# Weighting expert rows before an accumulating scatter, with a reordered router and double-buffered exponentials

## What is computed

```python
# differential attention: 4 heads, two 64-wide score maps each, 1024 keys
w = softmax(q1 @ k1.T * scale) - lam * softmax(q2 @ k2.T * scale)
o = rms_norm(w @ v, g_sub) * (1 - lam_init)
...
h = h + concat([oa, ob]) @ w_out
# mixture of experts: 32 experts in 4 groups, the best 2 of the best group for each token
a = rms_norm(h, g_ffn)
weights, experts = route(a @ w_rg, a @ w_re)          # [1024, 2]
y_e = (silu(a_e @ w1[e]) * (a_e @ w3[e])) @ w2[e]     # w1, w3: 1024x512, w2: 512x1024
h = h + sum over the two slots of weights * y_e
h = h + rms_norm(p @ w_ple, g_ple) * sigmoid(rms_norm(h, g_plg) @ w_plg)
# then two hybrid layers (retention and stick-breaking attention) and a last norm
```

## Time and profile before

| | us |
|---|---|
| median of 3 runs | 3491.62 (3491.36 to 3495.02) |
| profiled execution, its own time | 3490.98 |
| its span in the trace | 3489.2 |
| TensorE busy | 2927.1 (84%) |
| VectorE busy | 1540.2 (44%) |
| ScalarE busy | 1222.0 (35%) |
| GpSimd busy | 298.2 (9%) |

### The profile page before, as it was taken

One profiled execution on the slowest core, in us unless ns is written; L12 is line 12 of the kernel. 1 busy time (PEld: TensorE's weight loads), 2 busy tenths in 40 slices (PEclk: granted clock), 3 DMA queues, 4 the chain that ended last, 5 costly groups with the idle time before them and its releaser, 6 DMA issues. The chain is left out here.

```text
span 3489.2 us, 61320 instructions
## 1 busy us (share of the span) xinstructions
PE 2927.1 (84%) x22494; PEld 2278.4 (65%) x22494; DVE 1540.2 (44%) x2880; ACT 1222.0 (35%) x2193; POOL 298.2 (9%) x489
## 2 busy tenths in 40 slices
PE   7997875886966999999477999868877999868876
PEld 6785654665854888888365888754466888754455
DVE  3852666777222221222344421168844421058853
ACT  4332544666031110101243222258832222148841
POOL 0001641000002111111100000000000000000000
PEclk9998997898967999999788999979998999979988
DMA  5114543211346999999755222341044221160034
GB/s 181 66 72 162 136 129 105 63 35 65 99 147 225 386 394 393 392 394 395 249 189 175 94 96 72 121 141 34 10 157 160 103 99 72 66 205 19 25 121 163
DMA packets 246492, 541.80 MB, mean 155 GB/s; under 512 B 29904, under 2 KB 112656, under 8 KB 221680
## 3 DMA queue, kind: packets, MB, share of 16 engines
q1 hardware_dynamic: 216832, 460.21, 37.1%
q0 software_dynamic: 28544, 79.99, 6.9%
q10 hardware_dynamic: 1008, 0.20, 0.0%
HBM read 433.46 MB, written 107.79 MB: 155 GB/s over the span
## 5 line engine op out<-in xcount | busy, mean ns | idle before, releaser
L509 PE MATMUL ps<-in_wh,in_xh 128*128 (+1 forms) x1024 | 401.0, 392 | 0.0
L511 PE MATMUL ps<-in_wh,in_xl 128*128 (+1 forms) x1024 | 399.5, 390 | 0.0
L510 PE MATMUL ps<-in_wl,in_xh 128*128 (+1 forms) x1024 | 399.4, 390 | 0.0
L509 PEld LDWEIGHTS ps<-in_wh,in_xh 128*128 128x128 f32 x1024 | 193.1, 189 | 40.0
L510 PEld LDWEIGHTS ps<-in_wl,in_xh 128*128 128x128 f32 x1024 | 193.0, 188 | 39.8
L511 PEld LDWEIGHTS ps<-in_wh,in_xl 128*128 128x128 f32 x1024 | 192.8, 188 | 40.1
L1061 DVE TENSOR_TENSOR ex_hid<-ps,ex_act 32x128 f32<-32x128 f32 x96 | 28.2, 294 | 325.4 <-PE ps L1108 324.5
L509 PE MATMUL ps<-mix_in_wh,mix_in_xh 128*128 (+1 forms) x384 | 152.1, 396 | 9.0 <-DVE mix_in_out L426 5.4
L510 PE MATMUL ps<-mix_in_wl,mix_in_xh 128*128 (+1 forms) x384 | 149.9, 390 | 0.0
L511 PE MATMUL ps<-mix_in_wh,mix_in_xl 128*128 (+1 forms) x384 | 149.8, 390 | 0.0
L275 ACT COPY in_out<-ps 128x512 f32<-128x512 f32 x64 | 37.5, 587 | 249.0 <-PE ps L511 249.0
(11 more groups left out here) (408 smaller groups left out, 7318.9 us busy)
## 6 DMA issues: line engine op xcount, KB each, us to landing
ex_w_w1a<-in_w_dram SPq DMA_DIRECT2D x32, 1024.0 KB
ex_w_w1b<-in_w_dram SPq DMA_DIRECT2D x32, 1024.0 KB
ex_w_w3a<-in_w_dram SPq DMA_DIRECT2D x32, 1024.0 KB
ex_w_w3b<-in_w_dram SPq DMA_DIRECT2D x32, 1024.0 KB
ex_w_w2a<-in_w_dram SPq DMA_DIRECT2D x32, 1024.0 KB
ex_w_w2b<-in_w_dram SPq DMA_DIRECT2D x32, 1024.0 KB, 14.3
proj<-in_out SPq DMA_DIRECT2D x128, 256.0 KB, 2.0
da_w_ada<-in_w_ada_dram SPq DMA_DIRECT2D x32, 768.0 KB, 4.3
```

Of the source, the lines that this page charges most:

```text
L509: pe.matmul(o, xh[:, kt, tok], wb[0], start=(kt == 0), stop=False)
L510: pe.matmul(o, xh[:, kt, tok], wb[1], start=False, stop=False)
L511: last = pe.matmul(o, xl[:, kt, tok], wb[0], start=False, stop=(kt == KT - 1))
```

## The change

1. **Scatter that weights and adds.** The rows of `slot_rows` get a third word, the gate weight, laid into `tok` by VectorE. In the expert phase VectorE multiplies `y` by that word before it reports `y_out`, and the scatter goes to the token's row of `h1` itself with `compute_op=ADD` in place of a plain write to `slot_y`. `h1` gets 128 spare rows for the empty slots, filled once by the router phase.
2. **`ple_gate` without mixing.** The `mixed` mode is gone: no `ye` loads, no `mix`, no store of `h2`; `resid=h1`.
3. **Router.** All x tiles are loaded by SyncE, x[0] ahead of gain and weights and the other seven ahead of `pr` and `w_p`. The weights go to two contiguous tiles and GpSimd copies them into a cleared `wr` of 64 columns. The logits are made with `wr` stationary (64 columns) and `xt` moving (128 columns), even and odd kt on different halves of the partitions (`half_logits`); VectorE copies the halves, and a product with the constant `fold` adds and turns them (`join`). TensorE waits for all constants before the first of these. `turn_p(1..3)` stand behind the logits, weigh(1) ahead of the block table, and the scatter of the first slot starts without waiting for the second's.
4. **Differential attention.** Two sets of `e`, `total` and `inv`; TensorE runs score(0) and score(1) first and then score(t+2) ahead of tile t; VectorE's order becomes maxima(t+1), combine(t), invert(t), squares(t-2); the tile loops of ScalarE and VectorE are unrolled.

```diff
-            if mixed:
-                for t in range(NT):
...
-                    pool.dma_start(x[p][:], src[own, :]).then_inc(x_loaded[p], 16)
-                    if t >= 1:
-                        pool.wait_ge(x_mixed, t)
-                    for i in range(TOP_K):
-                        pool.dma_start(ye[i][:], k.slot_y[i * SEQ + t * P:i * SEQ + (t + 1) * P, :]).then_inc(ye_loaded, 16)
-                    if t >= 1:
-                        pool.dma_start(resid[(t - 1) * P:t * P, :], x[1 - p][:]).then_inc(x_saved[1 - p], 16)
...
-                dve.scalar_tensor_tensor(out=x[p][:], in0=ye[0][:], scalar=k.slot_w[:, 0, one], in1=x[p][:],
-                                         op0=ALU.mult, op1=ALU.add).then_inc(mid_mixed, 1)
...
-            sp.dma_start(wr[:, :, 0:N_GROUPS], w_rg.rearrange("(p k) n -> p k n", p=P)).then_inc(weights_loaded, 16)
-            sp.dma_start(wr[:, :, N_GROUPS:NL], w_re.rearrange("(p k) n -> p k n", p=P)).then_inc(weights_loaded, 16)
+            for q in range(XB):
+                sp.dma_start(x[q][:], src[q * P:(q + 1) * P, :]).then_inc(x_loaded[q], 16)
+                if q == 0:
+                    sp.dma_start(gain_b[:], row_to_all(gain, DM)).then_inc(gain_loaded, 16)
+                    sp.dma_start(w_group[:], w_rg.rearrange("(p k) n -> p k n", p=P)).then_inc(weights_loaded, 16)
+                    sp.dma_start(w_expert[:], w_re.rearrange("(p k) n -> p k n", p=P)).then_inc(weights_loaded, 16)
...
+            def half_logits(t):
+                pe.wait_ge(x_out, t + 1)
+                if t >= 2:
+                    pe.wait_ge(half_out, t - 1)
+                for kt in range(KT):
+                    part = slice(kt % 2 * HALF, (kt % 2 + 1) * HALF)
+                    last = pe.matmul(psL[t % 2][part, :], wr[:, kt, :], xt[t % 2][:, kt * P:(kt + 1) * P], start=(kt < 2), stop=(kt >= KT - 2))
+                last.then_inc(halved, 1)
+            def join(t):
+                pe.wait_ge(half_out, t + 1)
+                pe.matmul(ps_logit[:, t * NL:(t + 1) * NL], halves[t % 2][:], fold[:], start=True, stop=True).then_inc(logits, 1)
             turn(0)
-            pe.wait_ge(weights_loaded, 32)
+            pe.wait_ge(wr_done, 2)
+            pe.wait_ge(consts_loaded, 16 * 7)
...
-                pool.indirect_dma_start(out=k.slot_y[:, :], out_offset=bass.IndirectOffsetOnAxis(ap=row_own[:, 1:2], axis=0),
-                                        in_=y[:], in_offset=None).then_inc(stored, 16)
+                pool.indirect_dma_start(out=h[:, :], out_offset=bass.IndirectOffsetOnAxis(ap=row_own[:, 1:2], axis=0),
+                                        in_=y[:], in_offset=None, compute_op=ALU.add).then_inc(stored, 16)
...
-                dve.tensor_copy(y[:, 0:YM], psY[0:BR, 0:YM]).then_inc(y_out, 1)
+                dve.tensor_copy(y[:, 0:YM], psY[0:BR, 0:YM]).then_inc(y_copied, 1)
+                dve.wait_ge(y_copied, n + 1)
+                dve.wait_ge(row_loaded, 16 * (n + 1))
+                dve.tensor_scalar(y[:], y[:], row[:, 2:3].bitcast(F), None, ALU.mult).then_inc(y_out, 1)
...
                 score(NT * h, 0)
+                score(NT * h + 1, 1)
                 for t in range(NT):
                     i = NT * h + t
                     modulate(h, t)
-                    if t + 1 < NT:
-                        score(i + 1, t + 1)
+                    if t + 2 < NT:
+                        score(i + 2, t + 2)
...
-                    maxima(i + 1)
-                    combine(i + 1)
-                    squares(i, h, t)
-                    invert(i + 1)
+                    if t + 1 < NT:
+                        maxima(i0 + t + 1)
+                    combine(i0 + t, t)
+                    invert(i0 + t, t)
+                    if t >= 2:
+                        squares(i0 + t - 2, h, t - 2)
```

More of the change, by code:

```diff
@@ L356, in scale @@
                     dve.wait_ge(x_rs, t + 1)
-                    if mixed and (not isinstance(t, int) or t > 0):
-                        dve.wait_ge(x_turned, t)
-                    last = dve.scalar_tensor_tensor(out=xs[p][:], in0=x[p][:], scalar=rs[:, one], in1=gain_b[:],
+                    last = dve.scalar_tensor_tensor(out=x[p][:], in0=x[p][:], scalar=rs[:, one], in1=gain_b[:],
                                                     op0=ALU.mult, op1=ALU.mult)
@@ L673, in _ @@
                 take(t, t % 2)
[L674 to L679, removed]
+            for i in range(NT // 2):
+                act.wait_ge(p_turned, i + 1)
+                act.copy(pT[:, 2 * i:2 * i + 2, :], psP[i % 2].rearrange("p (t d) -> p t d", t=2)).then_inc(p_taken, 1)
+            act.wait_ge(consts_loaded, 16 * 7)
             act.dma_start(k.slot_rows.rearrange("(p b) a -> p b a", p=P), spare[:]).then_inc(spare_written, 16)
@@ L728, in _ @@
                     turn(t + 1)
-                if t % 2 == 1:
-                    pe.wait_ge(pr_loaded, 16)
-                    turn_p(t // 2)
-                pe.wait_ge(x_out, t + 1)
-                for kt in range(KT):
-                    last = pe.matmul(ps_logit[:, t * NL:(t + 1) * NL], xt[t % 2][:, kt * P:(kt + 1) * P], wr[:, kt, :],
-                                     start=(kt == 0), stop=(kt == KT - 1))
-                last.then_inc(logits, 1)
+                half_logits(t)
+                if t >= 1:
+                    join(t - 1)
+            pe.wait_ge(pr_loaded, 16)
+            turn_p(0)
+            join(NT - 1)
+            pe.wait_ge(l_taken, 1)
+            for i in range(1, NT // 2):
+                turn_p(i)
             pe.wait_ge(p_taken, NT // 2)
@@ L752, in _, with lay_halves @@
         def _(dve):
+            def lay_halves(t):
+                dve.wait_ge(halved, t + 1)
+                if t >= 2:
+                    dve.wait_ge(logits, t - 1)
+                dve.tensor_copy(halves[t % 2][:], psL[t % 2]).then_inc(half_out, 1)
             dve.wait_ge(gain_loaded, 16)
-            with dve.Fori(0, NT // XB) as j:
-                for q in range(XB):
-                    t = XB * j + q
-                    one = bass.ds(t, 1)
+            for t in range(NT):
+                    q, one = t, slice(t, t + 1)
                     dve.wait_ge(x_ss, t + 1)
@@ L863, in _, with expert_phase @@
                                    -3.0, None, ALU.add))
-            for t in range(1, NT):
+            for t in range(2, NT):
                 weigh(t)
-def expert_phase(nc, k, w1, w3, w2, after):
+def expert_phase(nc, k, w1, w3, w2, h, after):
     HK = KT // 2
@@ L884, in expert_phase @@
         wy = [s.sb(f"w_w2{n}", [P, HY, DM]) for n in "ab"]
[L885 removed]
+        idx, row, idx_own, row_own, nothing = (s.sb(n, [BR, 3], I32) for n in ("idx", "row", "idx_own", "row_own", "nothing"))
         copied = s.sem("copied")
```

200 lines of the change are left out of this document (96 added, 104 removed).

## The result

The changed kernel takes 3433.28 us (median of 4 runs, 3425.63 to 3439.64) against 3491.49 for the kernel before on the same chip (3485.82 to 3495.02): a ratio of 0.9835, 95% interval 0.9821 to 0.9849, 58 us less. The forecast was 19.4 us less. The changed kernel's profiled execution took 3431.25 us (span 3429.7).

The account below looks back on a forecast made before the run. It took the DMA engines to bound the experts and a chain of operations ple_gate. Terms of -42 (ple_gate), -16 (router), -5 (attention), +41.6 and +2 (experts) sum to -19.4, giving 3472 us; range 3450 to 3491, 8 in 10 3432 to 3512.

Parts of the forecast that it names:

- I take 1.3: Experts: the scatter's add makes each block 1.3 us longer, 32 x 1.3 = 41.6 us in all.
- Whatever is added to DMA work there lies on the path in full: Experts: the DMA engines set the 18.06 us period, so any added transfer work lengthens it by its whole cost.
- Both bounds for the price: Experts: the add's read per block, 1.15 us by the scatter's queue share or 1.0 us at the weights queue's rate.
- Tail, +2: End of the experts: a slower scatter and the extra multiplication are paid once, 2 us.
- Router, start, 9: Router: first logits wait for all seven constants, near 980 in place of 989.03, 9 us gained.
- ScalarE's 3.65 is the floor: Router loop: a tile takes between 3.65 and the old 5.4 us; 4.4 taken, 8 us gained over eight tiles.
- Router, behind the logits, 1 lost: Router: three `turn_p` ahead of `embed` delay the ranks 2 to 4 us, partly given back by weigh(1); net 1 us lost.
- Attention, -5: Differential attention: faster steady and last tiles outweigh a longer head start, 1.3 us a head, 5 us gained.
- ple_gate, -42: ple_gate: without mixing, six intervals of 7.9 in place of 12.7 us gain 29, an earlier tile 1 gains 13.
- rival B: Experts: the add's read is hidden, below 0.6 us a block; total 3431 to 3450 us, 3436 likeliest; chance 0.17.
- A: The forecast: the experts' add costs 0.6 to 1.9 us a block, all on the path; 3472 us, 3450 to 3491; chance 0.55.
- C: Experts: the add is dear, using up the gain at 1.9 us a block; at 3 us, 3527 us total; chance 0.2.

Follow-up runs that it names:

- e2_none: The changed kernel with the experts' scatter left out, 256 bytes sent in its place: 3398.71 us.
- r3_more: r2_form with eight further products of 128 moving columns in each router tile that nobody reads: 3449.30 us, ratio 0.9881.
- e3b_addplain: The changed kernel with a second, plain scatter to another tensor behind each accumulating one: 3463.6 us.
- e3_two: The changed kernel with a second accumulating scatter, to another tensor, behind each accumulating one: 3499.58 us.
- g1_oneload: The changed kernel with each expert block's slot words loaded once, into a table in SBUF, in place of twice: 3442.86 us, ratio 0.9873.
- r2_form: The changed kernel with the router's logits in their old form (xt stationary, 36 moving columns, no halves or join): 3450.25 us, ratio 0.9888.

## Why the prediction was wrong

The sign and the list of what each part does were right, but the 58 us lie three times as far from zero as the 19.4. The measured 3433.28 is below the forecast's own range of 3450 to 3491 and only 1 us inside the range for 8 in 10, 3432 to 3512. Two terms did most of it.

- **Experts, "I take 1.3".** The step that failed is "Whatever is added to DMA work there lies on the path in full", together with the mark-up on the price. An add costs 0.89 us where it can't hide, 0.74 in the late blocks of the changed kernel, and nothing in the first ones. Without the tail that is 18.1 us over 32 blocks, 0.57 a block, in place of 41.6. Both bounds for the price (1.15 and 1.0) were above the 0.89; the lower one, bytes at the rate of the weights queue, was nearer, and the 1.3 had no row behind it but a fear of the round trip. The row that spoke against "in full" was there: TensorE busy 179.0 of 180. A second bound so near takes part of any small addition. The two signs that were read as a bound of the DMA engines are none: in e2_none the share is 1.02 too and 3.6 pieces are always under way, while TensorE never waits. And the 3.4 us of the earlier trace rows are the weight load's; the matmuls lost 0.9 us there in ten blocks. The Trainium skill, "Collectives: The Full Stack", on the bandwidth ceiling, puts a collective's reduce at half of a copy's rate, 1.93 times as slow when measured. The runs here agree: 0.92 for a write and 0.89 more for the add, 1.97 times.
- **Tail, +2.** 4.0, from TensorE's last product (1680.85 before, 1656.39 after) to the next phase. The slower scatter and the multiplication, which the term counted, are 2.2 of it (1.3 and 0.9). The last scatter's own slower landing, 7.8 us from its issue to the next phase in place of 6.0, it left out.
- **Router, start, 9.** 9.1: right. It was held by the constants' last landing, as forecast.
- **Router, "ScalarE's 3.65 is the floor", 4.4 a tile.** This failed, and with it 14 of the 18.6 us: the loop gained 21.9 and not 8. ScalarE's operations of a tile (a square of 1.06, two small ones of 0.2, a copy of 1.0) are 2.5 us; the 3.65 held a wait of 1.17 us for transposes that TensorE did at the low clock. The changed loop runs at 2.7 us. And the low clock was taken as given. The old products took 3.46 us at 0.50; the change made the products shorter at that clock and lifted the clock as well, which r3_more shows apart from the amount of work.
- **Router, behind the logits, 1 lost.** 3.6 gained; 1.6 of it is the `embed` products that stand ahead of the ranks, 7.1 us at the high clock in place of 8.7.
- **Attention, -5.** -8.6. Both rates were right to 0.1 us. From the first maxima of a head to its last transposes the head start costs 6.7 to 7.4 us, more than the 5.7, and the intervals of a head gain 7.1 to 7.7 in place of 7.0. That leaves 1.0 us for the three heads of even pace together; in the trace of before the third head held two tiles of 8.7 and 7.2 us, and it gains 3.4. The other 4.2 us lie between a head's last transposes and the next head's first maxima, or the end of the phase, and a little ahead of the first head, where the forecast counted nothing; what makes them shorter is open. (The bound of 3 us lost for each of four heads is 12 and not 8; it entered no sum.)
- **ple_gate, -42.** -41.7. The six intervals gave 28.6 (29 forecast) and tile 1 comes 11.8 us sooner (13 forecast); that the total is nearer than its parts is luck.

The time is that of rival B (3431 to 3450, 3436 likeliest), and the 0.57 a block lies just under the 0.6 that divides B from A. But with the router and attention as forecast the time would be near 3455, in A's range: that B's figure was met to 3 us is luck. B's reason, that TensorE is itself 99% busy, was the right one. C is refuted by far: even the second accumulating scatter, write and add, costs 1.81 us a block.

## What to carry to other kernels

Ahead of pricing an addition to a "full" resource, ask how near the second bound is and how long the stage's lead lasts: here the experts paid a mean of 0.57 us a block of a price of 0.89. A busy share near 1 doesn't answer this; a run with the work taken away does. A floor for an engine is the sum of its operations' own durations, never the distance between two of its rows, which holds its waits. And a stretch in which TensorE is always busy at the low clock deserves a trial of the same products in another form before its instructions are counted.

## What the runs showed of the hardware

- Where the DMA engines are the bound, a scatter of 96 rows of 4 KB adds 0.92 us to the period for the write and 0.89 for the add (e3b_addplain, e3_two). The accumulating one lands in 9.1 us against 7.7, and GpSimd's issue takes 1.49 us against 0.94. The add is in the queue's time, not in its bytes.
- The share of the DMA engines is 1.02 in the experts of e2_none, where TensorE never waits, as in the changed kernel, where it does.
- 96 packets of 12 bytes for each block cost nothing that the period shows (g1_oneload, 18.8 us with and without them).
- In r2_form TensorE ran without a gap from 979 to 1009 us and its clock stayed at 0.50; in r3_more, with further products among the same ones, it was 1.00 in the same stretch. The amount of work a kernel gives TensorE and the time that it takes went in opposite directions.
